# Where the modulation products of a diffusion backbone stand: beside the norms, or behind the tiles of the mixer and the feed-forward

## What is computed

```python
mod = (silu(cond) @ w_mod + b_mod)            # 1024 x 6144 per layer
shift1, scale1, gate1, shift2, scale2, gate2 = split(mod, 6)
h = rms_norm(x, norm1_g) * (1 + scale1) + shift1
x = x + gate1 * mixer(h)                      # Fourier, attention, gated linear attention, w_out
h2 = rms_norm(x, norm2_g) * (1 + scale2) + shift2
x = x + gate2 * (relu(h2 @ w_ff1) ** 2 @ w_ff2)
```

## Time and profile before

| | us |
|---|---|
| median of 3 runs | 2166.69 |
| lowest, highest run | 2165.72, 2174.17 |
| the profiled execution's own time | 2172.02 |
| its span in the profile | 2170.2 |
| TensorE (PE) busy in that span | 2062.0 |
| VectorE busy | 951.7 |
| ScalarE busy | 751.7 |

### The profile page before, as it was taken

One profiled execution on the slowest core, in us unless ns is written; L12 is line 12 of the kernel. 1 busy time (PEld: TensorE's weight loads), 2 busy tenths in 40 slices (PEclk: granted clock), 3 DMA queues, 4 the chain that ended last, 5 costly groups with the idle time before them and its releaser, 6 DMA issues.

```text
span 2170.2 us, 33393 instructions
## 1 busy us (share of the span) xinstructions
PE 2062.0 (95%) x14480; PEld 1890.8 (87%) x14480; DVE 951.7 (44%) x1669; ACT 751.7 (35%) x1362; POOL 22.6 (1%) x45
## 2 busy tenths in 40 slices
PE   5999989999989999999989999999999899999997
PEld 3985688889979999999989766888999799999996
DVE  3245676333453343333443466942344533333334
ACT  5535544222353131322344355342232522222232
POOL 0000000000000000000000000000000000000000
PEclk9999999999999999999999999999999999999998
DMA  8210012453223233233342100125422222222221
GB/s 349 70 49 11 1 35 79 164 187 124 72 88 115 78 107 117 99 99 106 122 140 70 40 1 1 45 57 201 158 80 70 96 78 69 78 70 78 76 78 49
DMA packets 52002, 195.88 MB, mean 90 GB/s; under 512 B 6032, under 2 KB 6096, under 8 KB 51088
## 3 DMA queue, kind: packets, MB, share of 16 engines
q1 hardware_dynamic: 48384, 174.61, 24.1%
q0 software_dynamic: 3472, 19.14, 2.3%
HBM read 187.79 MB, written 5.93 MB: 89 GB/s over the span
## 4 chain that ended last, share of the span: by engine, by line
PE 86%; DVE 7%; ACT 3%; DMA 2%; issue 2%; SPq 0%; DVEq 0%; ACTq 0%
PE ps L533 68%; PE ps L635 3%; PE ps L781 2%; PE ps L644 2%; PE ps L757 2%; DMA w_raw<-in_stream 2%; PE ps L582 2%; PE ps L811 1%; PE ps L786 1%; DVE w_lo_parts L1265 1%; ACT scratch L1113 1%; DVE scratch L1538 1%; DMA scratch<-in_first 1%; PE ps L704 1%; PE ps L886 1%
## 5 line engine op out<-in xcount | busy, mean ns | idle before, releaser
L533 PE MATMUL ps<-h_hi_parts,w_hi_parts 128*128 128x320 f32 x2176 | 507.4, 315 | 18.1 <-DVE h_lo_parts L1265 11.8
L533 PE MATMUL ps<-h_lo_parts,w_hi_parts 128*128 128x320 f32 x2176 | 499.0, 311 | 0.0
L533 PE MATMUL ps<-h_hi_parts,w_lo_parts 128*128 128x320 f32 x2176 | 498.6, 311 | 0.0
L1265 DVE TENSOR_TENSOR w_lo_parts<-w_raw,w_hi_parts 128x512 fp32r<-128x512 f32 x464 | 299.0, 687 | 315.5 <-ACT w_hi_parts L981 314.8
L981 ACT CAST w_hi_parts<-w_raw 128x512 fp32r<-128x512 f32 x464 | 263.7, 617 | 497.8 <-PE ps L533 497.8
L533 PEld LDWEIGHTS ps<-h_hi_parts,w_hi_parts 128*128 128x128 f32 x2176 | 364.0, 189 | 48.6 <-DVE h_lo_parts L1265 20.9
L533 PEld LDWEIGHTS ps<-h_hi_parts,w_lo_parts 128*128 128x128 f32 x2176 | 366.4, 189 | 0.0
L533 PEld LDWEIGHTS ps<-h_lo_parts,w_hi_parts 128*128 128x128 f32 x2176 | 366.3, 189 | 0.0
L533 PE MATMUL ps<-hid_hi_parts,w_hi_parts 128*128 128x320 f32 x1280 | 293.3, 310 | 3.3 <-DVE merged L1580 3.3
L533 PE MATMUL ps<-hid_lo_parts,w_hi_parts 128*128 128x320 f32 x1280 | 292.0, 309 | 0.0
L533 PE MATMUL ps<-hid_hi_parts,w_lo_parts 128*128 128x320 f32 x1280 | 291.9, 309 | 0.0
(11 more groups left out here) (224 smaller groups left out, 1818.2 us busy)
## 6 DMA issues: line engine op xcount, KB each, us to landing
w_raw<-in_stream SPq DMA_DIRECT2D x312, 512.0 KB, 3.6
scratch<-in_first SPq DMA_DIRECT2D x10, 512.0 KB, 14.0
small_weights<-in_small POOLq DMA_DIRECT2D x2, 2048.0 KB, 10.4
h_scratch<-in_first SPq DMA_DIRECT2D x6, 512.0 KB, 16.9
x<-in_xT POOLq DMA_DIRECT2D x2, 1280.0 KB, 11.2
x<-in_xT POOLq DMA_DIRECT2D x8, 320.0 KB, 4.6
x_kept<-x POOLq DMA_DIRECT2D x8, 320.0 KB, 2.5
x<-x_kept POOLq DMA_DIRECT2D x8, 320.0 KB, 4.6
```

Source lines behind the costliest of these rows:

```text
L533: ins = mm(pair(o)[:, h, :], w[:, s % 2, k, :], a[:, k, h * HALF:(h + 1) * HALF], start=(first and n == 0), stop=(last and n == 2))
L1265: return tt(dst, full, hi.bitcast(F32), ALU.subtract)
```

## The change

Only the table `mods_after` is edited. The six pairs that stood beside the three norms go elsewhere, and the norms keep everything else.

```diff
@@ mods_after(s)
-    if MIX0 + 3 <= i < MIX0 + (15 if l == 0 else 13):
+    if MIX0 + 3 <= i < MIX0 + 15:
         return 1
-    if i in (OUT0 + KT - 1, PER - 1):
-        return 2 if i < PER - 1 or l == 0 else 0
-    if l == 0 and i in (FF0 + 1, FF0 + 2):
+    if l == 0 and FF0 + 1 <= i < FF0 + 5:
         return 1
-    if l == 0 and FF0 + 2 * KT <= i < FF0 + 7 * KT:
+    if l == 0 and FF0 + 12 <= i < FF0 + 60:
         return int((i - FF0) % 4 == 1)
```

## The result

| | before | after |
|---|---|---|
| median of 20 runs, us | 2168.64 | 2178.06 |
| lowest, highest run, us | 2163.02, 2174.17 | 2170.44, 2183.93 |
| ratio to before, 95% interval | 1 | 1.0046, 1.0036 to 1.0056 |
| span of the profiled execution, us | 2170.2 | 2175.2 |

The change costs 0.46%, or 10.0 us (7.8 to 12.1). I had said 7.2 us and a time of 2173.9. The ratios leave out two executions far off the rest, one of before (2307.52 us) and one of extra_six (5150.31 us), and since the second is the one that was traced, extra_six has no trace that can be compared.

A forecast was written before the change was run, and what follows sets the result against it. The prediction took TensorE, busy for 2062.0 of 2170.2 us, to bound the kernel. Its terms −0.5 + 3.4 + 2.0 + 2.0 + 0.3 gave +7.2 us on the runs' median 2166.69, so 2173.9 us, range 2168 to 2182.

The forecast's parts named there:

- predicted 3.4: Layer 0's pairs moved behind FF0+3 and FF0+4: running cost plus waits for loads, +3.4 us, between 2.0 and 5.5.
- two pairs for which I had 2.0: Two pairs from the norm between the layers, moved behind single feed-forward tiles: 1.0 each without wait, +2.0 us.
- predicted 0.5: Unit 11's turn leaves its place behind the first two products of layer 1's feed-forward, which gives back 0.5 us.
- 1.0 a pair: A pair of modulation matmuls in a full TensorE stream lies in the chain with its whole length, 1.0 us, without wait.
- the late start between the layers, −0.48: At the norm between the layers the product can start at 1114.49 instead of 1114.97 without the pair: −0.48 us.
- the other end of this term: If blocks and not the start pace the two products between the layers, the −0.48 is partly lost, up to 0.
- Clock. I take 0, since the fall is set by the idle time ahead of the second pair.: TensorE's lower clock at the three norms costs nothing more without pairs: 0, with +3 us as the upper end.
- The second part of the clock term: The low clock may last longer into the products behind the norms: 1.0 us a norm, 3.0 for three, as upper end.
- B: Rival: the load ring chokes and three new pairs each wait 1.2 us, 3.6 on top, 2177.5 us; chance 0.12.
- C: Rival: the clock stays low through a norm's first two products, +12.0 us in one place, 2185.9 us; chance 0.05.
- D: Rival: moved pairs hide in waits of their new places, leaving only −0.5 and +0.3, 2166.5 us; chance 0.08.
- The 0.5% that I took as the least a measurement could tell: For the whole kernel, about 0.5%, 10.8 us, is what a measurement can tell from no change.

The follow-up runs named there:

- extra_six: Before's table untouched, plus copies of six pairs, result unused, where the change puts them; +5.4 us over before, and +8.0 when run again for its trace.
- norms_bare: Before's table, with the six pairs beside the norms neither loaded nor multiplied; 2169.88 us, +2.4 us against before.
- second_kept: Against before, each norm's first pair runs behind the mean square and its second goes to FF0+3, FF0+57 or layer 1's mix tile 13; 2173.63 us, +5.4.
- first_kept: Against before, each norm's first pair stays ahead of the mean square, its second goes to FF0+3, FF0+57 or layer 1's mix tile 13; 2169.97 us, +2.6.
- after_fill: The changed kernel with eight matmuls on resident tables in each norm, result unused; 2177.58 us, +8.9 us against before.
- spread: Against before, the six pairs stay in the norms and pairs that wait for loads are set apart; 2156.61 us, −10.4, and when run again −9.3.
- before_look: The kernel before, unedited, run once more for a second trace; one run, 2166.83 us.

## Why the prediction was right, and where it wasn't

**Right: the direction, the size within the range, and the way.** The pairs were free in the norms inside the layers, no norm got shorter, and the six pairs cost their time where they went. By the stretches, FF0+2 to FF0+8 grew by 3.7 (predicted 3.4). The rest of that feed-forward grew by 3.3: two pairs for which I had 2.0, and unit 8's turn at 0.9, which moved there from layer 1. All kernels run the same main matmuls in the same order, so in layer 1 one can compare when the same matmul starts. From the last product of layer 0 to the end of the mixer after loses 1.3 us on before, but 0.9 of low clock between 1240 and 1385 us, in code that is the same, is to before's disadvantage there (two of after's three traces lack it, both traces of before have it). Without it the change costs 2.2: two pairs 2.4, unit 11's turn 0.9, unit 8's turn −0.6, waits −0.4. The first tiles of layer 1's feed-forward gave back 0.3 (predicted 0.5). Sum 8.9 us.

**Mis-sized: the pair.** The term "1.0 a pair" was read from the pair's own piece of the chain. The price is the longer period, 29.36 against 28.17, 1.19; six times 0.19 is 1.1 us. extra_six_2 shows it apart from the rest.

**Mis-sized: the late start between the layers, −0.48.** The first product does start earlier behind the mean square, 9.12 us and not 9.53, but the two products end no earlier. The last row of the two, before and after:

```profile
1130.85 0.46 PE L533 MATMUL ps<-h_hi_parts,w_lo_parts 128*128 128x320 f32 x2
```

```profile
1131.08 0.46 PE L531 MATMUL ps<-h_hi_parts,w_lo_parts 128*128 128x320 f32 x2
```

Counted from the mean square (1105.37 and 1105.60) both stand at 25.48. The blocks and not the start pace the products, as I had put it at the other end of this term, and it is 0. With 1.1 and 0.5 the predicted 7.2 becomes 8.8, against the 8.9 of the stretches.

**Failed: "Clock. I take 0, since the fall is set by the idle time ahead of the second pair."** I looked only at the second pair and the products behind the norm. The loss is ahead of it: without the *first* pair TensorE waits 1.96 and not 0.96 for VectorE's sum, and the mean square, which everything waits for, then often runs at 1.2 GHz. In the traces with that idle time (after three times, norms_bare, second_kept) 8 of 15 norms were late, by 0.91 to 1.70 us; in those with work ahead (before twice, first_kept, extra_six_2, after_fill, spread twice) none of 21. Mean over the 15: 11.8 / 15 = 0.8 us a norm, 2.4 us an execution (1.9 in after's own three traces). 8.9 + 2.4 = 11.3, against 10.0 (7.8 to 12.1) and 10.2 (6.9 to 13.2) measured. The traces as a whole say about the same: from the mean square of the first norm to the last product after's three lost 12.3, 8.7 and 14.2 us on the first trace of before and before_look 1.9, a difference of the means of 10.8.

The trace of before showed this step before anything ran, and I passed over it. The last norm of the program has no pair in any kernel:

```profile
2153.28 2.44 PE L603 MATMUL ps<-merged,tables 128*128 128x320 f32 x4 [2.03 <-DVE merged L1305]
2155.51 1.88 PE L606 MATMUL ps<-merged,tables 128*128 128x320 f32 x4
```

After 2.03 us of waiting its mean square took 4.11 us, at a mean clock of 0.59, where those with a pair ahead took 2.42. In 11 of the 12 traces it took 3.28 to 4.11 (2.42 in norms_bare). It costs all kernels alike, so it is no part of the 10.0.

The second part of the clock term, products starting at 1.2 GHz, is there as well, but in before too: in before_look the stretch that ends at the third low part of layer 1 was 2.1 us longer than in the trace of before. I can't say that the change made it larger.

**The rivals.** B (every pair waits) was wrong: FF0+3 and layer 1's mix tiles 13 and 14 had no wait. C (low clock through both first products) didn't occur; in after's traces no low stretch of a norm reached further than 6.5 us into them (8.2 in after_fill). D (hidden in the new places) was wrong for the six, though spread shows that such places exist behind the last mix tiles. The 0.5% that I took as the least a measurement could tell was too coarse: the interval is 0.1% to either side, and the change lies clear of it.

**Open:** which norm of an execution is late. It changes from run to run of the same kernel. In the 8 late ones the granted clock fell 0.06 to 1.4 us behind the start of the mean square, in the 7 others without work ahead 5.0 to 6.7 us behind it, when it was over. Why it fell sooner in one than in the other no run here was made to show.

## What to carry to other kernels

Price small work moved into a full stream by the period with and without it, not by its own row; and spread pieces whose loads reuse a slot that a neighbour frees late, rather than bunching them (here −0.45%). Small work that fills a wait just ahead of a short step on which everything depends can be worth something besides its own time (here 0.8 us a norm on average). Where the same program reaches the same point at times 7 us apart, compare stretches between fixed points, over several traces. And when a change takes work away from a place, look in the trace of before for a place that already lacks it.

## What was unexpected of the hardware

- With 1.96 us without work ahead of it, the mean square ran wholly or in part at the lower clock in 8 of 15 norms, and with 2.03 us in the last norm of 11 of 12 traces. With 0.96 us of waiting behind a pair it never did (0 of 18), nor with 0.24 us in after_fill's three norms. Its eight instructions together then took up to 4.1 us (1687.83 to 1691.93), not 2.4.
- A good part of the spread between runs goes with the granted clock. Over the 20 runs of after time and mean granted clock correlate at −0.83; the fastest, 2170.44 us, had 0.987, and the slowest, 2183.93, had 0.980.
- Filling the norms with matmuls raised the mean granted clock to 0.987 in the profiled execution of after_fill (0.983 to 0.987 in after's three), but not the speed by more than can be measured. Where the blocks of a norm, 1.86 us apart, set the pace, a low clock of 3.1 us in the first products cost nothing.
